# Two lent slots for split weights in four stretches, and a new order of units at the joints of the products

## What is computed

```python
def first_block(x, p, ...):
    u = rms_norm(h, ln_pre_mix)
    proj = u @ w_in                  # conv, moba, z, ga, gb are its columns
    ...                              # attention and gated delta rule -> y_a, y_b
    merged = sigmoid(gate_a) * (y_a @ w_proj_a) + sigmoid(gate_b) * (y_b @ w_proj_b)
    h = h + rms_norm(merged @ w_out, ln_post_mix)
    f = rms_norm(h, ln_pre_ffn)
    f = (silu(f @ w_ffn_gate) * (f @ w_ffn_up)) @ w_ffn_down          # ffn 1, down 1
    h = h + rms_norm(f, ln_post_ffn)
    e = rms_norm(p @ w_ple, ln_ple)
    return h + sigmoid(h @ w_ple_gate) * e

def second_block(x, mem, ...):
    proj = rmsnorm(x, g_mix_pre) @ w_in_2                             # in2
    mix = concatenate([diff_attention, pooled]) @ w_out_2             # out2
    x = x + rmsnorm(mix, g_mix_post)
    xq = rmsnorm(x, g_x_pre) @ w_xq;  kv = rmsnorm(mem, g_mem) @ w_xkv
    x = x + rmsnorm(cross_attention(xq, kv) @ w_xo, g_x_post)
    hf = rmsnorm(x, g_ffn_pre)
    return x + rmsnorm((silu(hf @ w_gate) * (hf @ w_up)) @ w_down, g_ffn_post)
```

## Time and profile before

| what | us |
|---|---|
| median of three runs | 1015.26 |
| lowest and highest | 1014.17, 1015.35 |
| time of the profiled execution | 1014.69 |
| its span | 1012.9 |
| TensorE busy | 977.6 |
| POOL busy | 741.6 |
| ACT busy | 512.6 |
| DVE busy | 366.5 |

### The profile page before, as it was taken

How to read it: one execution, slowest core, us unless ns; L and a number is a source line. 1 busy time by engine, 2 the same in 40 slices (tenths; PEclk the granted TensorE clock), 3 DMA queues, 4 the chain that set the end, 5 groups by cost and what they waited for, 6 DMA issues and landing times.

```text
span 1012.9 us, 15323 instructions
## 1 busy us (share of the span) xinstructions
PE 977.6 (97%) x6004; PEld 826.2 (82%) x6004; DVE 366.5 (36%) x840; ACT 512.6 (51%) x759; POOL 741.6 (73%) x592
## 2 busy tenths in 40 slices
PE   5999999999999999999999998999989999999997
PEld 5988889988888876878898876899868878888885
DVE  5677524676524235112122244243252161111103
ACT  5476624464524445455444455585455356544441
POOL 6767642877632876989996966878757369998892
PEclk9999999999999999999999999999999999999999
DMA  8546232555423665667765645655545247766551
GB/s 265 175 132 197 88 122 64 168 151 160 123 88 100 214 206 166 202 189 209 208 192 159 189 150 181 224 184 169 164 158 173 67 144 228 209 199 192 177 180 41
DMA packets 76752, 167.37 MB, mean 165 GB/s; under 512 B 8348, under 2 KB 13704, under 8 KB 76552
## 3 DMA queue, kind: packets, MB, share of 16 engines
q1 hardware_dynamic: 71296, 156.40, 50.2%
q10 hardware_dynamic: 5384, 9.99, 3.0%
HBM read 165.32 MB, written 1.05 MB: 164 GB/s over the span
## 4 chain that ended last, share of the span: by engine, by line
PE 82%; POOL 6%; ACT 5%; DVE 4%; issue 2%; DMA 1%; DVEq 0%; ACTq 0%
PE L L483 19%; PE L L485 18%; PE L L484 18%; POOL w_lo L472 6%; PE L L841 2%; PE L L842 2%; PE L L843 2%; ACT w_hi L1225 2%; PE Q L485 2%; PE Q L483 2%; PE Q L484 2%; PE Q L1010 1%; PE Q L698 1%; PE Q L992 1%; DMA raw<-in_w_ffn_gate 1%
## 5 line engine op out<-in xcount | busy, mean ns | idle before, releaser
L472 POOL TENSOR_TENSOR w_lo<-raw,w_hi 128x512 fp32r<-128x512 f32 x588 | 741.4, 1300 | 251.1 <-ACT w_hi L1225 250.7
L1225 ACT CAST w_hi<-raw 128x1024 fp32r<-128x1024 f32 x294 | 305.3, 1054 | 263.5 <-PE L L485 112.3
L483 PE MATMUL L<-w_hi,uH 128*128 128x512 f32 (+1 forms) x768 | 306.8, 399 | 12.9 <-POOL w_lo L472 7.2
L485 PE MATMUL L<-w_hi,uL 128*128 128x512 f32 (+1 forms) x768 | 296.6, 386 | 0.0
L484 PE MATMUL L<-w_lo,uH 128*128 128x512 f32 (+1 forms) x768 | 296.1, 386 | 0.0
L483 PEld LDWEIGHTS L<-w_hi,uH 128*128 128x128 f32 x768 | 144.3, 188 | 51.9 <-POOL w_lo L472 11.2
L485 PEld LDWEIGHTS L<-w_hi,uL 128*128 128x128 f32 x768 | 144.3, 188 | 29.9
L484 PEld LDWEIGHTS L<-w_lo,uH 128*128 128x128 f32 x768 | 144.6, 188 | 26.3 <-issue 0.5
L483 PE MATMUL L<-w_hi,hH 128*128 128x512 f32 x176 | 69.0, 392 | 0.0
L485 PE MATMUL L<-w_hi,hL 128*128 128x512 f32 x176 | 68.6, 390 | 0.0
L484 PE MATMUL L<-w_lo,hH 128*128 128x512 f32 x176 | 68.5, 389 | 0.0
(11 more groups left out here) (335 smaller groups left out, 1259.0 us busy)
## 6 DMA issues: line engine op xcount, KB each, us to landing
raw<-in_w_in SPq DMA_DIRECT2D x88, 512.0 KB, 3.6
raw<-in_w_ffn_gate SPq DMA_DIRECT2D x22, 512.0 KB, 3.7
raw<-in_w_ffn_up SPq DMA_DIRECT2D x22, 512.0 KB, 3.6
raw<-in_w_ffn_down SPq DMA_DIRECT2D x22, 512.0 KB, 3.7
raw<-in_w_gate SPq DMA_DIRECT2D x22, 512.0 KB, 4.2
raw<-in_w_up SPq DMA_DIRECT2D x22, 512.0 KB, 4.1
raw<-in_w_down SPq DMA_DIRECT2D x22, 512.0 KB, 3.5
raw<-in_w_out SPq DMA_DIRECT2D x16, 512.0 KB, 4.2
```

Of the source, the lines that this page charges most:

```text
L472: last = nc.gpsimd.tensor_tensor(w_lo[:, n % SPLIT, cc], raw[:, n % RAW, cc], w_hi[:, n % SPLIT, cc].bitcast(F32), ALU.subtract)
L483: mm(dst, sH, wH, start=start, stop=False)
L485: return mm(dst, sL, wH, start=False, stop=stop)
L1225: copy(w_hi[:, u % SPLIT, :], raw[:, u % RAW, :]).then_inc(w_hi_there, 1)
```

## The change

Slots are given out by a plan, `SLOT` and `BEFORE`, in place of n % 6: in four stretches of the program two more slots lie in memory that is free there. They are called SCAN (from unit 7 of `proj_a` to unit 4 of `ffn 1`'s fifth step), GATE (unit 19 of `down 1` to the end of `in2`), OUT (unit 6 of `out2` to `ffn 2`'s first step) and MEMORY (unit 4 of `xo` to the end). A cast waits for the last user of its own slot, eight units back in the stretches. ACT gets a wait at each of the first three entries, and one in `down 1`. `SPLIT` itself, and with it every place of a cast, stays. `HEAD` becomes 6 and `TAIL` 5: unit 5 of tile 0 goes ahead of tile 1, and five units of tile 1 are left to the tail. The next step's first turn goes ahead of the last three pieces. `skewed_columns` takes the second matrix's first unit after two units of the first. `kept(0, 1)` goes ahead of `hi_half(0, 1)`, and for `ffn1` and `mix2` `root` goes ahead of `lo_half`.

```diff
-HEAD = 5
-TAIL = 4
+HEAD = 6
+TAIL = 5
...
+    OPENED = {SCAN: NUMBER[("proj_a",), 7], GATE: NUMBER[("down", 1), 19], OUT: NUMBER[("out2",), 6], MEMORY: NUMBER[("xo",), 4]}
+    CLOSED = {SCAN: LAST["ffn", 1, 4], GATE: LAST["in2", 2], OUT: LAST["ffn", 2, 0], MEMORY: len(UNITS) - 1}
+    LENT = {SPLIT: (SCAN, MEMORY), SPLIT + 1: (SCAN, MEMORY), SPLIT + 2: (GATE,), SPLIT + 3: (GATE,), SPLIT + 4: (OUT,), SPLIT + 5: (OUT,)}
...
+        free_slots = list(range(SPLIT)) + [s for s, whens in LENT.items() if any(OPENED[o] <= n <= CLOSED[o] for o in whens)]
+        slot = min(free_slots, key=lambda s: newest.get(s, -1))
+        SLOT.append(slot)
+        BEFORE.append(newest.get(slot, -1))
...
-                        if last and (j, c) == (k_tiles - 1, 1):
+                        if last and (j, c) == (k_tiles - 2, 1):
                             last()
...
                 for j in range(4):
                     piece(j, 0, 1)
+                wait_low(source, 0, 1)
+                piece(4, 0, 0)
                 if turns(source):
                     turn_half(source, 1, 0)
                 elif source == ("cross",):
                     cross_values(1)
-                wait_low(source, 0, 1)
-                for c in range(2):
-                    piece(4, 0, c)
+                piece(4, 0, 1)
+                for j in range(5, HEAD):
+                    for c in range(2):
+                        piece(j, 0, c)
                 wait_low(source, 1, 0)
...
-                for j in (2, 3):
+                for j in range(2, KD - TAIL):
...
-                for j in range(4):
-                    if j == 1:
-                        turn_half(source, 0, 1)
-                    elif j == 2:
-                        wait_low(source, 0, 1)
-                    column_unit(first[0], first[1] + j, first_banks, tiles=(0,))
+                column_unit(first[0], first[1], first_banks, tiles=(0,))
+                turn_half(source, 0, 1)
+                column_unit(first[0], first[1] + 1, first_banks, tiles=(0,))
                 bank_free(source, 0, 1)
                 column_unit(second[0], second[1], second_banks, tiles=(0,))
+                wait_low(source, 0, 1)
+                for j in range(2, 4):
+                    column_unit(first[0], first[1] + j, first_banks, tiles=(0,))
                 turn_half(source, 1, 0)
...
-                    if u >= SPLIT:
-                        act.wait_ge(w_used, u - SPLIT + 1)
-                    copy(w_hi[:, u % SPLIT, :], raw[:, u % RAW, :]).then_inc(w_hi_there, 1)
+                    if BEFORE[u] >= 0:
+                        act.wait_ge(w_used, BEFORE[u] + 1)
+                    opened = ENTRY.get(u)
+                    if opened == SCAN:
+                        act.wait_ge(*PE(("scan", 1), "o", 1))
+                        act.wait_ge(*VE(("scan", 1), "sum", 1))
+                    elif opened == GATE:
+                        act.wait_ge(*VE(("e",), "e", 3))
+                    elif opened == OUT:
+                        act.wait_ge(*VE(("dnorm",), "da", 2 * GH - 1))
+                    copy(halves[SLOT[u]][0], raw[:, u % RAW, :]).then_inc(w_hi_there, 1)
...
                         split_past(step, 2)
+                        act.wait_ge(w_used, CLOSED[SCAN] + 1)
...
-                    hi_half(step, 0, 1)
                     if pre:
                         kept(what, 0, 1)
+                    hi_half(step, 0, 1)
...
-                    lo_half(step, 0, 1)
-                    root(what, 1)
+                    if what in ("ffn1", "mix2"):
+                        root(what, 1)
+                        lo_half(step, 0, 1)
+                    else:
+                        lo_half(step, 0, 1)
+                        root(what, 1)
```

## The result

The changed kernel takes 1027.46 us (median of four runs, 1023.75 to 1030.34) beside 1015.31 for the kernel before on the same chip: ratio 1.012, interval 1.0083 to 1.0158. It is slower by 12 us where 6 were forecast. The median lies 2.5 us above the forecast's own range (1017.5 to 1025) and half a microsecond above the wider one for eight in ten (to 1027). The profiled execution took 1025.76 us around a span of 1024.0, so 11.1 us more span than before.

The account below looks back on a forecast made before the run. TensorE, busy 977.6 of 1012.9 us, was taken to bound the kernel: matmuls plus gaps at seams between products. Seam terms summed to +6.1 us on 1015.26, about 1021; range 1017.5 to 1025, eight in ten 1016.5 to 1027.

Parts of the forecast that it names:

- Part 1: Two slots more, casts unmoved in ACT's order: saves 0.45 us in `xo`, helps `proj_b`; casts behind a turn's copy stay late.
- rival (a): The slots were the limit: weights five to seven ready when wanted, 994 us; with partial forms (1005 to 1013) chance 0.10.
- the slots lift the second only: A cast waits for its place in ACT's program and its slot; more slots remove only the wait for the slot.
- Part 2: Five units held in row products: unit 6 loses 3.05 us (`xq` 4.1); `ple_gate` +2.3, `w_out` +1.3, `xq` +2.0.
- Part 3: Last turn three pieces ahead: entry waits of next products go; -0.9 `proj_b`, -1.0 each `ple_gate` and `xq`, -1.5 `ffn 2` with `xo`.
- the four terms: Savings at the entries: `proj_b` -0.9, `ple_gate` -1.0, `xq` -1.0, `cross` and `xo` to `ffn 2` -1.6.
- Part 4: Column steps: the fifth unit, wanted sooner, loses 3.05 us; +1.7 in `ffn 1`, +1.6 in `in2`, +1.7 in `ffn 2`.
- the clock's term of the sum: Clock loss behind the six new pauses: nothing in the sum or its range, left to rival (c).
- rival (c): Granted clock falls to 1.2 GHz behind each of six pauses, 1.5 to 2 us each, about 1031 us; chance 0.10.

Follow-up runs that it names:

- e2: The changed kernel with one or two casts more at places earlier in ACT's order; 995.39 us, ratio 0.981.
- e4: The lent slots alone, with the old orders of TensorE, ACT and DVE; 1013.39 us, ratio 0.9981 to the kernel before.
- e5: The changed kernel's new orders with six slots throughout, no lent ones; 1054.51 us, ratio 1.0383.
- e1: The changed kernel with useless matmuls in its six long pauses, twelve in each and sixteen in `xq`; 1019.57 us, ratio 1.005.
- e8: The kernel of e2 with the next step's first turn ahead of the last piece again, instead of three ahead; 999.67 us.
- e7: The kernel before with twelve pauses, TensorE waiting for a clearing and two products on DVE, in three steps of each ffn; 1075.74 us.
- e12: The kernel before with six pauses, TensorE waiting for five clearings on DVE, in three steps of each ffn; 1047.45 us.
- e3: The changed kernel with the old order in the column steps; 1016.05 us, ratio 1.0008 to the kernel before.
- e11: The kernel before with twelve pauses, TensorE waiting for one clearing on DVE, in three steps of each ffn; 1027.28 us.

## Why the prediction was wrong in size and right in kind

**Part 1** holds. ACT's and POOL's rows show the cast behind the copy, and e2 shows the cure. Its rival (a) gave 994 as the time if the weights came when wanted; e2, in which they do, measured 995.4. They do so by the casts' places; that the slots were the limit, as (a) has it, e4 refutes. But the wording "the slots lift the second only" was too narrow: e5 shows that they also lift what queues behind a waiting cast. It did no harm to the sum, which never took the slots away.

**Part 2** holds. In `ple_gate`, the one product whose clock stayed up, the stalls are 1.04 and 0.50 for units 4 and 5 (forecast 1.0 and 0.6), 2.97 at unit 6 (3.05), 0.99 at unit 7 (1.05), and the product is +2.3 as forecast. In `xq` unit 6 lost 4.00 (4.1), but unit 7 nothing where 1.05 were counted, and in `w_out` unit 7 came 0.41 late instead of 1.05: TensorE was at half its clock just then, and POOL caught up. So part of the slow stretch hid in a wait that the sum had counted, and that `xq` is only 0.3 above its +2.0 is luck: the missing wait and the slow rows cancel. In e1, at full clock, both stalls are there (idle 0.82 and 0.81) and both products as forecast.

**Part 3** holds: the entries' waits on `uL` are gone, the four terms came to -0.9, -1.5, -0.9 and -2.2 for -0.9, -1.0, -1.0 and -1.6 (with `cross`), and e8 measured the turn's place at 4.3. The -1.5 has half a microsecond of luck in it: the wait behind the slow transfer in `ffn 1` was 0.66 us in this execution and 1.21 before. The -2.2 has TensorE's 0.4 us on ACT's `xv` in it, which the sum had left out and which is gone.

**Part 4** holds for the wait: 3.05, 3.08 and 3.07 lost at the fifth unit of the three column steps, forecast 3.05. Its terms of +1.7, +1.6 and +1.7 are 1.5 to 1.8 too low each, as the clock fell behind all three.

**The step that failed is the clock's term of the sum.** The sum counts every matmul behind the six new pauses at full clock, puts nothing for the clock and no bound for it into the range, and leaves it to rival (c) at 0.10. The runs show 5 to 8 us in its place (between the medians 7.9, 1027.46 against e1's 1019.57), and 4.7 for all the rest. The mechanism and its price per pause were written down in (c): 1.5 to 2 us behind each, 9 to 12 in all, 1031. It happened at five of six, for 1.2 to 1.6 each. Between the forecast's 1021 and (c)'s 1031 the kernel measured 1027.5, and its runs reach from 1023.8 to 1030.3. The chance of 0.10 rested on one row, 8 to 13 us, where TensorE stood idle for 2.6 us at full clock. Two things were wrong with that. The row was shorter than any of the six. And it wasn't the same situation: from 5.0 to 8.4 us TensorE was busy for 0.84 of 3.4 us, whereas ahead of each new pause it had been fully busy for 4 us and more. Whether that second difference matters no run here isolates, but e7's two pauses of 2.50 us behind dense matmuls, no longer than the row's, were followed by slow rows; what the row couldn't do was speak against pauses of 3 to 4 us. Of the Trainium skill ("TensorE: Matmul & The Clock Gate", section "Why this matters for your kernels") the prediction had cited that long idle gaps send the array back to half its clock. The traces agree: 0.50 to 0.58 behind five of six pauses here, and 0.50 to 0.71 in the 4 to 6 us behind each of e12's six. Here a page's rule should have outweighed a single unlike row, and a range is there to reach such a case.

**What stays open.** Which pauses lower the clock isn't settled. That of `ple_gate`, 2.97 us behind 4.4 us of full work, did not in the profiled execution, and the runs of the changed kernel differ by 6.6 us with clocks of 0.985 to 0.994, so not every execution has as many slow stretches; in e3's it is `ple_gate` that has one. Nor does the length of a pause decide by itself. Four of e7's twelve were followed by full clock, two of 2.4 us (492.45, 949.61) but also two of 3.46 (513.21, 970.35), while the two of 2.50 (521.29, 978.42) were followed by 0.64 and 0.63. Behind that of 521.29 and that of 949.61:

```profile
521.40:526.00 4.60, 4.60 (x18) 3.95 (x19) 1.38 (x2) 2.12 (x3) 1.43 (x2) 0.63 0.27 99
...
949.60:954.00 4.40, 4.39 (x24) 3.78 (x25) 1.38 (x2) 2.48 (x4) 1.60 (x2) 1.00 0.30 107
```

## What to carry to other kernels

More slots help an engine that works in order only if its order lets the work start earlier: look at what stands ahead of the late instruction in its queue, and move the instruction along with the slots (here 1.5 us from the slots alone, 9.5 more from the places of the casts, 8.5 more from the orders). Count a pause of TensorE of 3 us or more at its length and another 1.2 to 1.9 us for the clock (behind five of six in the changed kernel, and on average behind e12's six), with a chance of its own, and reach for it in the range. Of e7's twelve, 2.4 to 8.7 us long, eight had slow rows behind them and four none; e11's of 1 us cost only themselves. An order with fewer gaps on paper can be the slower one until its inputs come earlier: the new orders cost 14 us with the casts where they were (1013.4 to 1027.5) and are worth 8.5 with the casts early (1003.9 to 995.4).

## What the hardware showed

- **Useless matmuls paid.** Twelve of them in each of five pauses and sixteen in the sixth made the kernel 7.9 us faster, by keeping the granted clock at 0.999 instead of 0.991. The profile page's line of TensorE's clock, in 40 slices of some 26 us, shows nines throughout in the changed kernel; only windows cut at the pause show the fall.
- **A product on DVE waits for POOL.** With both inputs and the output in SBUF it took 8.53 us instead of 0.69 while POOL subtracted without a break; clearings beside the same kind of POOL work took 0.48. The Trainium skill ("SBUF — State Buffer", section "SBUF: two separate sides") has it that a DVE operation with two SBUF inputs and a GpSimd operation that reads SBUF take a shared pair of ports by an exclusive lock. The traces agree that one waits while the other works, and add that for how long isn't fixed: the DVE side waited through eight instructions of POOL once, and in e7 came in after each one (1.64 us for a product).
- **A slow clock is partly free** where another wait follows: 0.41 us in `w_out` and none in `xq` at unit 7, beside 0.99 in `ple_gate`.
